# A two-layer encoder trunk in split float32: feature tiles of the split input 1,032 bytes apart in place of 1,024

## The reference

```python
for l in range(DEPTH):                       # DEPTH = 2
    xn = rmsnorm(h, norm_mix[l])
    u = xn @ w_in[l]
    branches = (attention(u), conformer(u), ssd(u), fourier(u))
    h = h + sum(sigmoid(xn @ w_gate[l, i] + b_gate[l, i]) * br_i) @ w_out[l]
    xn = rmsnorm(h, norm_ffn[l])
    h = h + (swiglu(xn, ...) if l % 2 == 0 else moe_swiglu(xn, ...))
    h = h + sigmoid(h @ ple_gate[l]) * (p[l] @ ple_proj[l])
return rmsnorm(h, final_norm)
```

## Time and profile before

| | us |
|---|---|
| median of three runs | 2148.46 |
| the three runs | 2146.51, 2148.52, 2148.46 |
| span of the profiled execution | 2147.9 |
| TensorE busy with matmuls | 2118.1 (99%) |
| TensorE loading columns | 1894.9 (88%) |
| VectorE busy | 1684.0 (78%) |
| ScalarE busy | 1323.0 (62%) |

### The profile page before, as it was taken

One profiled execution on the slowest core, in us unless ns is written; L12 is line 12 of the kernel. 1 busy time (PEld: TensorE's weight loads), 2 busy tenths in 40 slices (PEclk: granted clock), 3 DMA queues, 4 the chain that ended last, 5 costly groups with the idle time before them and its releaser, 6 DMA issues.

```text
span 2147.9 us, 37284 instructions
## 1 busy us (share of the span) xinstructions
PE 2118.1 (99%) x13622; PEld 1894.9 (88%) x13622; DVE 1684.0 (78%) x2373; ACT 1323.0 (62%) x1864; POOL 24.2 (1%) x45
## 2 busy tenths in 40 slices
PE   9999999999999999999999999999999999999997
PEld 8999999999999999999888888888888888888886
DVE  4998766655557998766689888988888899888885
ACT  5545654444435455654477777777777777777773
POOL 0000100000000000100000000000000000000000
PEclk9999999999999999999999999999999999999998
DMA  7534436364354434443489899998989899898971
GB/s 253 188 118 164 146 130 234 138 214 178 130 201 164 159 118 160 158 178 138 177 318 367 320 353 340 352 364 326 363 338 350 333 350 371 325 357 338 345 302 73
DMA packets 74965, 533.19 MB, mean 248 GB/s; under 512 B 8655, under 2 KB 8655, under 8 KB 11000
## 3 DMA queue, kind: packets, MB, share of 16 engines
q1 hardware_dynamic: 72620, 525.04, 64.6%
q0 software_dynamic: 2048, 6.29, 1.6%
q10 hardware_dynamic: 204, 0.54, 0.1%
HBM read 530.74 MB, written 1.10 MB: 248 GB/s over the span
## 4 chain that ended last, share of the span: by engine, by line
PE 95%; DVE 3%; ACT 1%; DMA 1%; issue 0%; SPq 0%; DVEq 0%; ACTq 0%
PE ps L896 28%; PE ps L898 28%; PE ps L897 28%; PE ps L559 4%; PE ps L1091 1%; PE ps L1120 1%; PE ps L850 1%; PE ps L878 1%; PE ps L762 1%; PE ps L865 1%; DMA constants_sb<-constants 0%; DVE rstd L1735 0%; DVE wlo L2127 0%; PE ps L571 0%; DVE xn L1741 0%; DMA ring<-w_ple 0%
## 5 line engine op out<-in xcount | busy, mean ns | idle before, releaser
L2127 DVE TENSOR_TENSOR wlo<-ring,whi 128x1024 fp32r<-128x1024 f32 x746 | 872.6, 1219 | 144.0 <-ACT whi L1562 143.6
L1562 ACT ACTIVATE whi<-ring 128x1024 fp32r<-128x1024 f32 x746 | 749.3, 1055 | 139.9 <-PE ps L898 130.4
L896 PE MATMUL ps<-whi,xhi 128*128 128x512 f32 (+1 forms) x1160 | 439.4, 379 | 0.7 <-DVE xlo L2253 0.7
L898 PE MATMUL ps<-whi,xlo 128*128 128x512 f32 (+1 forms) x1160 | 430.1, 371 | 0.0
L897 PE MATMUL ps<-wlo,xhi 128*128 128x512 f32 x904 | 356.9, 395 | 0.0
L896 PE MATMUL ps<-xhi,whi 128*128 128x256 f32 x960 | 273.4, 285 | 2.6 <-DVE gt L2149 1.4
L897 PE MATMUL ps<-xlo,whi 128*128 128x256 f32 x960 | 268.9, 280 | 0.0
L898 PEld LDWEIGHTS ps<-whi,xlo 128*128 128x128 f32 x1160 | 219.0, 189 | 40.4
L898 PE MATMUL ps<-xhi,ring_lo 128*128 128x256 f32 x896 | 252.1, 281 | 0.0
L896 PEld LDWEIGHTS ps<-whi,xhi 128*128 128x128 f32 x1160 | 219.4, 189 | 35.4 <-DVE xlo L2253 1.1
L897 PEld LDWEIGHTS ps<-wlo,xhi 128*128 128x128 f32 x904 | 170.3, 188 | 35.8
(11 more groups left out here) (307 smaller groups left out, 3823.5 us busy)
## 6 DMA issues: line engine op xcount, KB each, us to landing
ring<-w_experts SPq DMA_DIRECT2D x340, 1024.0 KB, 5.0
ring<-w_mixers SPq DMA_DIRECT2D x114, 1024.0 KB, 5.0
ring<-w_dense SPq DMA_DIRECT2D x33, 1024.0 KB, 4.8
ring<-w_ple SPq DMA_DIRECT2D x10, 1024.0 KB, 4.9
bias<-bias_rows POOLq DMA_DIRECT2D x8, 256.0 KB, 7.0
cvfa<-bias_rows POOLq DMA_DIRECT2D x8, 256.0 KB, 5.2
constants_sb<-constants SPq DMA_DIRECT2D x1, 1048.0 KB, 9.0
h<-x_in SPq DMA_DIRECT2D x1, 1024.0 KB, 4.8
```

Of the source, the lines that this page charges most:

```text
L896: pe.matmul(dst, lhs[0], rhs[0], start=first, stop=False, skip_group_check=True)
L898: return pe.matmul(dst, lhs[1], rhs[0], start=False, stop=last, skip_group_check=True)
L1562: act.activation(whi[:, slot, :], ring[:, j % RING, lo:lo + UNIT], ACT.Copy).then_inc(s_wh, 1)
L2127: dve.tensor_tensor(wlo[:, slot, :], ring[:, j % RING, lo:lo + UNIT], whi[:, slot, :], ALU.subtract).then_inc(s_wl, 1)
```

## The change

A constant `STEP = 2` is added, and `xhi` and `xlo` are allocated with 258 columns per tile, of which the first 256 are used as before. Tile k now begins 1,032k bytes behind the buffer's start in place of 1,024k. Each of the two buffers is 64 bytes longer, so `xlo` moves by 64 bytes and all that is allocated behind it by 128. No instruction is added, removed or moved, and no wait.

```diff
+STEP = 2
-        xhi = sb("xhi", [P, KT, SEQ], F32R)
-        xlo = sb("xlo", [P, KT, SEQ], F32R)
+        xhi = sb("xhi", [P, KT, SEQ + STEP], F32R)[:, :, 0:SEQ]
+        xlo = sb("xlo", [P, KT, SEQ + STEP], F32R)[:, :, 0:SEQ]
```

## The result

| | before | after |
|---|---|---|
| median, us | 2150.05 (8 runs, 2146.51 to 2153.30) | 2156.27 (8 runs, 2154.23 to 2159.01) |
| ratio, 95% interval | | 1.0027 [1.0018, 1.0036] |
| span of the profiled execution, us | 2147.9 | 2154.5 |
| the profiled execution's own time, us | | 2156.59 |

The eight runs before are the three of the forecast and five more. The forecast was 2145.6 us. The time rose by 6.2 us, near the rival in which streams pay for a crooked start (+8.5 us).

What follows compares the result with a forecast made beforehand. TensorE's pace from one matmul to the next was taken as the bound. Terms of +4.8 - 7.1 - 0.6 = -2.9 us took the span from 2147.9 to 2145.0; with 0.6 us added, 2145.6 us, range 2134 to 2163.

Steps and rivals of the forecast that it cites:

- the rival in which streams pay for a crooked start: Slower rival: any streamed start not at phase 0 costs 2.2 ns in 3,864 matmuls, +8.5 us, 2157 us; chance 0.20.
- The bound: Whole kernel: TensorE busy 2118.1 of 2147.9 us, so only its pace between matmuls can move the time.
- Step 1: Input streamed, phases (start address by 64 bytes) differing now: tile 4 +1.2 us, six other tiles +3.6 us.
- step 3: Input streamed through query_key_high_x and gate_high_b, one common phase now: together -0.6 us.
- Step 2: Input loaded under 512 streamed columns in the experts: tile 4 -1.8 us, six other tiles -5.3 us.
- Step 4: Input loaded under 256 streamed columns: 0, ends +-1.3 us, since a start moved by 4 bytes cost nothing.
- the rival in which streamed operands pay too: Both kinds pay: each operand off its line, streamed or loaded, costs 5.2 ns, +38.5 us, 2187 us; chance 0.08.
- Step 5: VectorE and ScalarE accessing tiles that no longer adjoin: 0; if gaps cost, under 1 us at stage heads.
- Products without the input: Products without xhi and xlo keep phase and pace; the dense down product must stay at 5.76 us.
- The signs to look for: Dense up product: 11.31 us if streams don't care, 11.52 if all tiles but one go to 120.0 ns.
- no placement could matter: Rival from TensorE's two independent read ports: placement does nothing, 2148.5 us; chance 0.13.

Runs made afterwards that it cites:

- e4_experts32: Kernel before with the experts' split tokens in columns 8 to 135 of each tile, so their loaded operand starts at phase 32; ratio 0.9998.
- e1_shift: Against the kernel before: tiles stay 1,024 bytes apart, each buffer 64 bytes longer at its end, so xlo moves 64 bytes and all behind it 128; ratio 1.0008.
- e7_high_only: Against the kernel before: only xhi gets the spacing of 1,032 bytes, xlo keeps 1,024; ratio 0.9994.
- e2_start8: Against the kernel before: tiles stay 1,024 bytes apart, all eight start 8 bytes later, buffers end 64 bytes later; ratio 1.0067, 2165.3 us.
- e8_step1: Against the kernel before: tiles of xhi and xlo lie 1,028 bytes apart; ratio 1.0019.
- e9_bench_quiet: Bench of the kernel's own matmul patterns alone, other engines idle, streamed or loaded start varied; streamed means by place 119.1, 121.0, 120.7 and 116.7 ns.
- e12_start12: Against the kernel before: tiles stay 1,024 bytes apart, all start 12 bytes later; ratio 0.9996.
- e5_bench: Bench of TensorE alone, blocks of 72 matmuls from buffers at varied offsets; 256 columns streamed at offset 0 took 120.0 ns, at 4 bytes 123.1.
- e13_start12_experts16: All tiles start 12 bytes later, and the experts' tokens one column later so their loaded operand starts at 16 bytes; ratio 0.9985 against the kernel before.
- e6_experts8: Kernel before with the experts' split tokens in columns 2 to 129, so their loaded operand starts at 8 bytes; ratio 0.9972, 2145.59 us.

## Why the prediction was wrong

- **The bound** was right: TensorE is 99% busy in both traces, and no other engine took over.
- **Step 1, streamed input** (+4.8 us, with step 3 +4.2): right in sign and nearly in size, +5.8 us measured. But not for its reason, so the size is in part luck. Tile 4, which trades phases, should have gone up by 2.2 ns and went up by 0.6; most of the loss sits in the odd tiles, +1.2 to +2.0 ns each, and these start 8 bytes into 16. The count was off as well: `ring_lo` lies at phase 0, so 736 more streamed matmuls, the third ones of most groups, had one common phase before. With them in step 3 the two steps give +2.6 us in place of +4.2. In the trace before, streams through `ring_lo` run at 118.4 ns and not at the 120.0 of `query_key_high_x`; that was a sign against the phase as the reason.
- **Step 2, loaded input in the experts** (-7.1 us) is the step that failed: +0.7 us measured. I took the difference of 5.2 ns between up and down product for one of phase. e4_experts32 gives both operands the same phase and changes nothing; tile 4 went from 232.1 to 235.8 ns and not down by 5.2. Without this term the sum would have been +4.2 us, against +6.2 in the runs. Why the down product is faster stays open.
- **Step 3** (-0.6 us) has the right sign where I can see it: a group of three with `query_key_high_x` went from 359.8 to 356.3 ns, 128 x 3.5 = -0.4 us.
- **Step 4, loaded under 256 columns** (0 +-1.3 us): +0.6 us, inside. But its row misled me: the start moved by 4 bytes that costs nothing was one of a loaded operand, and I used it against the rival in which streamed operands pay too.
- **Step 5** was right: VectorE's and ScalarE's busy time rose by under 1 us each.
- **Products without the input** kept their pace in the dense part, as foretold, but not in every kernel: the experts' down product went from 228.6 to 229.5 ns in the shift alone. The phase by 64 bytes was the wrong quantity, or not the only one, since the shift keeps all phases and moved the experts' up product by 1.6 ns a matmul. Against the shift alone, the change loses in both kinds: 119.08 against 118.31 ns streamed (4,992 x 0.77 = 3.8 us), 233.23 against 231.48 loaded (2,712 x 1.75 = 4.7 us). So half of the loss against that control is in loaded operands, and no run explains that half. The sums of the two profiles differ by only 6.62 - 2.56 = 4.1 us, since other kinds go the other way and the shift's profile stood at half clock for 23.9 us among the matmuls, that of the change for 13.7.
- **The rival that came nearest** is the slower one, with its place (the streamed operand) right and its rule wrong: it charges every start off phase 0 with 2.2 ns. In the runs starts at 12 and 16 bytes cost nothing on the mean, and starts 4 and 8 bytes into 16 cost from 0.5 ns (e7_high_only) to 2.7 (e2_start8). That its +8.5 us lies near +6.2 is in part luck.
- **The signs to look for**: the dense up product took 11.45 us, between the 11.31 and 11.52 that were named. With one tile of eight left at 117.8 ns the second number should have been 11.49; 11.52 is all tiles at 120.0.

The Trainium skill (Advanced Engine Details and Errata, "SBUF Cachelines") speaks of 16-byte lines. The period of 16 bytes in e8_step1 (118.4, 120.1, 120.9, 117.5 ns) and in e9_bench_quiet agrees with that size. Its condition of two accesses to a line, by which the half line would be free, does not match: a start with two words left in its line (8 bytes) cost 2.7 ns per matmul in e2_start8, and one with a single word left (12 bytes) cost nothing in e12_start12. The Trainium skill (SBUF — State Buffer, "Who interferes with whom") has TensorE's two read ports independent. The prediction drew from it that no placement could matter, which the runs refute: with nothing else at work the loaded offset alone moved the pace from 120.0 to 115.6 ns in e5_bench. Whether the two reads disturb each other or the load has a price of its own, no run separates.

Open: why 12 bytes are free and 4 and 8 are not; why the price of 8 bytes depends on the operand loaded and nearly vanishes in e7_high_only; what sets the experts' pace between 230.5 and 233.5 ns (it repeats with the placement to 0.1 ns, but I found no rule); and why the same section of a bench can run at two paces 1.1 ns apart. A start at 4 bytes was tried only in tiles 1 and 5 of e8_step1 and in the benches, never in a full kernel by itself.

## What to carry to other kernels

When TensorE runs back to back, keep the streamed operand's start on a multiple of 16 bytes: pad rows of split float32 by four words, not two (1.0027 became 0.9986; half of that came from loaded operands, so it has to be measured). A difference of pace between two places of one kernel isn't a price until one operand alone was moved; e4_experts32 would have corrected the forecast's sign. Moving buffers that the change doesn't speak of is itself worth 1.6 ns a matmul in the experts (e1_shift), so a layout change is measured beside its shift alone. And two profiles are compared with the time at half clock in view: it made up the whole difference between the streams of e12_start12 and e13_start12_experts16.

## What the runs showed of the hardware

- On the mean over the kernel, a streamed split-float32 operand of 256 columns costs about 2 ns more per matmul when it starts 4 or 8 bytes past a multiple of 16, and nothing at 12: 120.1, 120.9, 117.5 against 118.4 ns in tiles 1, 2, 3 and 0 of e8_step1; 121.0, 120.7, 116.7 against 119.1 ns in e9_bench_quiet. The mean hides much: in e2_start8 the price of 8 bytes was 0.5 to 4.7 ns by the operand loaded, in e7_high_only 0.5 ns.
- The same placement gives the same pace: streams that lie alike differ by at most 0.05 ns between kernels (117.92, 117.92, 117.87). Moving buffers by 64 and 128 bytes changes it (233.08 to 231.48 ns for the experts' loads in e1_shift).
- A loaded operand at 8 bytes doesn't pay that: 230.5 against 233.1 ns in e6_experts8.
- The pace of one fixed pair of shapes (128 columns loaded, 256 streamed) ranged from 113.3 to 123.1 ns with nothing but the two starts changed (e5_bench).
